# One decoder layer on one NeuronCore: w_down over all eight PSUM banks, with seven block products in place of eight for six of sixteen pairs of contraction tiles

## The reference, cut to what matters

```python
x = x + merged @ w_out                                  # (256, 2048)
hn = rms_norm(x, norm_mlp)                              # gain, and a factor per token
x = x + jnp.square(jax.nn.relu(hn @ w_up)) @ w_down     # w_up (2048, 8192), w_down (8192, 2048)
```

## Time and profile before

| | before |
|---|---|
| median of three runs | 1338.79 us (1338.76 to 1339.06) |
| the profiled execution: span from the first to the last instruction | 1337.1 us |
| TensorE busy | 1333.2 us, 6034 matmuls |
| VectorE busy | 961.8 us |
| ScalarE busy | 652.0 us |
| GpSimd busy | 14.9 us |
| granted TensorE clock, mean over the core's activity | 1.000 of full |
| read from memory | 256.46 MB, 193 GB/s |

### The profile page before, as it was taken

How to read it: one execution, slowest core, us unless ns; L and a number is a source line. 1 busy time by engine, 2 the same in 40 slices (tenths; PEclk the granted TensorE clock), 3 DMA queues, 4 the chain that set the end, 5 groups by cost and what they waited for, 6 DMA issues and landing times.

```text
span 1337.1 us, 16355 instructions
## 1 busy us (share of the span) xinstructions
PE 1333.2 (100%) x6034; PEld 1109.3 (83%) x6034; DVE 961.8 (72%) x1333; ACT 652.0 (49%) x797; POOL 14.9 (1%) x30
## 2 busy tenths in 40 slices
PE   9999999999999999999999999999999999999999
PEld 7988888888888888888888888888888888888887
DVE  6788699777487875999787878444546878764453
ACT  6656544656445444454545454343335454543332
POOL 0101000000000000000000000000000000000000
PEclk9999999999999999999999999999999999999999
DMA  9656565555556755564656565555566665555552
GB/s 317 206 172 220 190 203 164 186 186 164 183 161 217 252 197 184 186 220 163 215 189 198 182 213 180 201 188 191 196 196 197 191 192 188 191 197 198 197 191 95
DMA packets 131829, 259.35 MB, mean 194 GB/s; under 512 B 4366, under 2 KB 7484, under 8 KB 131516
## 3 DMA queue, kind: packets, MB, share of 16 engines
q1 hardware_dynamic: 131740, 258.57, 58.5%
q10 hardware_dynamic: 32, 0.01, 0.0%
HBM read 256.46 MB, written 2.10 MB: 193 GB/s over the span
## 4 chain that ended last, share of the span: by engine, by line
PE 99%; DMA 0%; SPq 0%; DVE 0%; issue 0%
PE ps L1100 31%; PE ps L1102 31%; PE ps L1101 31%; PE ps L1190 1%; PE ps L1171 1%; PE ps L1139 1%; PE ps L1135 1%; PE ps L1137 1%; PE ps L1145 0%; DMA rows<-in_x_dram 0%; PE ps L1210 0%; PE ps L1227 0%; PE ps L1209 0%; PE ps L1238 0%; PE ps L1120 0%; PE ps L1254 0%
## 5 line engine op out<-in xcount | busy, mean ns | idle before, releaser
L697 DVE TENSOR_TENSOR w_lo<-raw,w_hi 128x1024 fp32r<-128x1024 f32 (+1 forms) x477 | 581.0, 1224 | 337.7 <-ACT w_hi L429 333.5
L429 ACT ACTIVATE w_hi<-raw 128x1024 fp32r<-128x1024 f32 (+1 forms) x477 | 503.8, 1061 | 584.8 <-PE ps L1102 575.6
L1100 PE MATMUL ps<-w_hi,xT 128*128 128x512 f32 x1088 | 425.8, 391 | 0.0
L1102 PE MATMUL ps<-w_hi,xT 128*128 128x512 f32 x1088 | 423.5, 389 | 0.0
L1101 PE MATMUL ps<-w_lo,xT 128*128 128x512 f32 x1088 | 423.3, 389 | 0.0
L1102 PEld LDWEIGHTS ps<-w_hi,xT 128*128 128x128 f32 x1088 | 204.2, 188 | 42.8
L1100 PEld LDWEIGHTS ps<-w_hi,xT 128*128 128x128 f32 x1088 | 204.3, 188 | 41.9
L1101 PEld LDWEIGHTS ps<-w_lo,xT 128*128 128x128 f32 x1088 | 204.3, 188 | 41.7
L1100 PE MATMUL ps<-w_hi,branch 128*128 128x512 f32 x384 | 149.4, 389 | 0.0
L1101 PE MATMUL ps<-w_lo,branch 128*128 128x512 f32 x384 | 149.4, 389 | 0.0
L1102 PE MATMUL ps<-w_hi,branch 128*128 128x512 f32 x384 | 149.4, 389 | 0.0
(11 more groups left out here) (199 smaller groups left out, 582.0 us busy)
## 6 DMA issues: line engine op xcount, KB each, us to landing
raw<-in_w_in_dram SPq DMA_DIRECT2D x73, 1024.0 KB, 5.1
raw<-in_w_up_dram SPq DMA_DIRECT2D x64, 1024.0 KB, 5.8
raw<-in_w_down_dram SPq DMA_DIRECT2D x64, 1024.0 KB, 5.0
raw<-in_w_out_dram SPq DMA_DIRECT2D x16, 1024.0 KB, 5.1
raw<-in_w_branch_b_dram SPq DMA_DIRECT2D x8, 1024.0 KB, 5.0
raw<-in_w_branch_a_dram SPq DMA_DIRECT2D x8, 1024.0 KB, 5.1
raw<-in_w_in_dram SPq DMA_DIRECT2D x4, 1040.0 KB, 8.7
rows<-in_x_dram SPq DMA_DIRECT2D x1, 2048.0 KB, 10.1
```

The lines of the kernel that those rows point to most:

```text
L429: act.activation(dst[:, k % RING, :, :], src[:, k // 2, KH * (k % 2):KH * (k % 2) + KH, :], ACT.Copy).then_inc(hi_made, 1)
L697: dve.tensor_tensor(lo[:, k % RING, :, :], src[:, k // 2, KH * (k % 2):KH * (k % 2) + KH, :], hi[:, k % RING, :, :].bitcast(F32), ALU.subt ...
L1100: pe.matmul(o, hi, w_hi[:, s, i, :], start=first, stop=False)
L1102: last = pe.matmul(o, lo, w_hi[:, s, i, :], start=False, stop=end)
```

## The change

The down stage of each half f is done in two blocks n of 1024 columns instead of four of 512. A block has 16 pairs of contraction tiles, taken in a written order (`ORDER`), and SyncE loads one pair of tiles by 1024 columns (1 MB) per slot. TensorE adds up into all eight banks: four of the block's own (two token halves by two column halves), four shared ones for the other kind of pair.

Ten of the pairs are whole pairs: two steps of one tile by 1024 columns, 12 matmuls each, as many as before. The six others (`SEVEN`) take the pair of tiles, the two token halves and the two column halves as a 2 by 2 block product and do it with seven block products instead of eight: four steps with 6, 3, 6 and 6 matmuls. For this the weights need four sums (w1 - w0, w3 - w1, w3 less the first, w2 less the third). GpSimd makes them with three TENSOR_TENSOR instructions per pair (two sums of 512 in one of 1024 elements, and two of 512), into `w_diff` and in place in the raw slot. ScalarE and VectorE split 1024, 512, 1024 and 1024 elements for the four steps; steps 2 and 3 wait for GpSimd (`diff_made`). The features need four sums too: VectorE makes them (five instructions of 128 elements per pair, in the up stage), and ScalarE and VectorE split them (two instructions each).

The four shared banks are combined and added into `rows` by VectorE (`add_shared`), and the own banks by `add_own`. The factor of the token is no longer applied at these adds but at the Relu, as its square root (`x2_r`, from GpSimd), and the Relu is two instructions of 512 instead of one of 1024. The loops of the MLP are written out. The end of the last block is cut as before, with two 256-wide pieces last. The diff, cut:

```diff
 B_UP = B_OUT + NN
-FB = 16
+SEVEN = (3, 5, 7, 9, 11, 13)
+ORDER = ((0, 1, 2, 4, 3, 6, 5, 8, 7, 10, 9, 12, 11, 13, 14, 15), (0, 3, 1, 5, 2, 7, 4, 9, 6, 11, 8, 13, 10, 12, 14, 15))
+PARTS = [[4 if i in SEVEN else 2 for i in ORDER[n]] for n in range(2)]
+DOWN = sum(PARTS[0]) + sum(PARTS[1])
+FB = 8 + DOWN // 8
...
+        w_diff = gate_f[:, 0:1024]
+        part_sums = gate_f.rearrange("p (a n) -> p a n", n=N)
...
+        def step_of(f, n, at, part=0):
+            return 8 * (B_UP + FB * f + 8) + (sum(PARTS[0]) if n else 0) + sum(PARTS[n][:at]) + part
...
+                for n in range(2):
+                    for at, i in enumerate(ORDER[n]):
+                        k = at % RAW
+                        if n == 0 and at < RAW:
+                            sp.wait_ge(lo_made, 8 * (B_UP + FB * f + 7) + 2 * k + 2)
+                        else:
+                            was = (n, at - RAW) if at >= RAW else (0, 16 + at - RAW)
+                            sp.wait_ge(lo_made, step_of(f, *was) + PARTS[was[0]][was[1]])
+                        sp.dma_start(raw[:, k, :, :].rearrange("p (a b) n -> p a (b n)", b=2),
+                                     w_down_t[:, 32 * f + 2 * i:32 * f + 2 * i + 2, 2 * N * n:2 * N * n + 2 * N])\
...
+                    before = None
+                    for at, i in enumerate(ORDER[n]):
+                        if i not in SEVEN:
+                            continue
+                        k, made = at % RAW, diffs_before(f, n, at)
+                        q = raw[:, k, :, :]
+                        pool.wait_ge(landed[k], 16 * (B_UP + 16 * f + 8 + 4 * n + at // RAW) + 16)
+                        if before is not None:
+                            pool.wait_ge(lo_made, before + 1)
+                        else:
+                            if n == 0:
+                                pool.wait_ge(up_squared, 8 * f + 8)
+                            if n == 1 or f == 1:
+                                pool.wait_ge(shared_read, 2 * f + n)
+                        pool.tensor_tensor(diffs, q[:, 1:4:2, :], q[:, 0:2, :], ALU.subtract).then_inc(diff_made, 1)
+                        pool.wait_ge(diff_made, made + 1)
+                        link(pool.tensor_tensor(q[:, 1, :], q[:, 3, :], diffs[:, 0, :], ALU.subtract))
+                        pool.wait_ge(lo_made, step_of(f, n, at) + 1)
+                        pool.tensor_tensor(q[:, 2, :], q[:, 2, :], q[:, 1, :], ALU.subtract).then_inc(diff_made, 1)
+                        before = step_of(f, n, at, 2)
...
+            def down_hi(f, s):
+                n, at, part = place_of(f, s)
+                g, k = step_of(f, n, at, part), at % RAW
+                flat = raw[:, k, :, :].rearrange("p t n -> p (t n)")
+                dst = w_hi[:, g % RING, :, :].rearrange("p t n -> p (t n)")
+                if PARTS[n][at] == 2:
+                    src = flat[:, 1024 * part:1024 * part + 1024]
+                else:
+                    src = (flat[:, 1024:2048], flat[:, 0:N], w_diff, flat[:, N:N + 1024])[part]
+                if part == 0:
+                    act.wait_ge(landed[k], 16 * (B_UP + 16 * f + 8 + 4 * n + at // RAW) + 16)
+                elif part >= 2:
+                    act.wait_ge(diff_made, diffs_before(f, n, at) + part - 1)
+                act.wait_ge(w_used, g - RING + 1)
...
+                    for m in range(M):
+                        last = act.activation(up_pos[:, N * m:N * m + N], ps[:, 4 + 2 * u + m, :], ACT.Relu,
+                                              scale=x2_r[:, m:m + 1])
+                    last.then_inc(up_read, 1)
...
+                if at == 0 and 2 * j - 1 in SEVEN:
+                    q, t = SEVEN.index(2 * j - 1), 4 * j - 2
+                    act.wait_ge(pair_sum, len(SEVEN) * f + q + 1)
+                    act.activation((branch, merged)[t // 16][:, t % 16, 0, P:S], sums[:, 0, :], ACT.Copy)
+                    act.activation(sum_ops(2 * j - 1)[:, :, 0, :], sums[:, 1:4, :], ACT.Copy).then_inc(pair_hi, 1)
...
+                        if 8 * blk0 + i == step_of(f, n, last_shared(n), 3) + 3:
+                            act.wait_ge(w_used, step_of(f, n, last_shared(n), 3) + 1)
+                            act.activation(part_sums[:, 0, :], ps[:, SHARED[n], :], ACT.Copy).then_inc(first_kept, 1)
...
+                if at == 7 and 2 * j + 1 in SEVEN:
+                    a11, a21, a12, a22 = (ps[:, 2 * u + 1, P * c:P * c + P] for c in range(4))
+                    link(dve.tensor_copy(sums[:, 3, :], a21))
+                    dve.tensor_tensor(sums[:, 2, :], a11, sums[:, 3, :], ALU.subtract)
+                    link(dve.tensor_tensor(sums[:, 0, :], sums[:, 3, :], a22, ALU.add))
+                    link(dve.tensor_tensor(sums[:, 1, :], sums[:, 0, :], a11, ALU.subtract))
+                    dve.tensor_tensor(sums[:, 3, :], a12, sums[:, 1, :], ALU.subtract).then_inc(pair_sum, 1)
+                if at == 1 and 2 * j - 1 in SEVEN:
+                    q, t = SEVEN.index(2 * j - 1), 4 * j - 2
+                    dve.wait_ge(pair_hi, len(SEVEN) * f + q + 1)
+                    a, ops = (branch, merged)[t // 16][:, t % 16, :, P:S], sum_ops(2 * j - 1)
+                    dve.tensor_tensor(a[:, 1, :], sums[:, 0, :], a[:, 0, :].bitcast(F32), ALU.subtract)
+                    dve.tensor_tensor(ops[:, :, 1, :], sums[:, 1:4, :], ops[:, :, 0, :].bitcast(F32),
+                                      ALU.subtract).then_inc(pair_lo, 1)
...
+            def add_shared(f, n, late_part):
+                b, r0, r1 = SHARED[n], out_rows(0, n), out_rows(1, n)
+                if not late_part:
+                    dve.wait_ge(first_kept, 2 * f + n + 1)
+                    link(dve.tensor_tensor(part_sums[:, 2, :], part_sums[:, 0, :], ps[:, b + 2, :], ALU.add))
+                    dve.tensor_tensor(part_sums[:, 1, :], part_sums[:, 2, :], ps[:, b + 1, :], ALU.add)
+                    link(dve.tensor_tensor(part_sums[:, 3, :], part_sums[:, 2, :], ps[:, b + 3, :], ALU.add))
+                    link(dve.tensor_tensor(r1.rearrange("p (a n) -> p a n", a=2), r1.rearrange("p (a n) -> p a n", a=2),
+                                           part_sums[:, 3, :].unsqueeze(1).to_broadcast([P, 2, N]), ALU.add))
+                else:
+                    dve.tensor_tensor(r1[:, N:2 * N], r1[:, N:2 * N], ps[:, b + 1, :], ALU.add)
+                    link(dve.tensor_tensor(r0, r0, part_sums[:, 0:2, :].rearrange("p a n -> p (a n)"), ALU.add))
+                    dve.sem_inc(shared_read, 1)
...
+            def add_own(f, n):
+                dve.wait_ge(w_used, step_of(f, n, 15, 1) + 1)
+                for m in range(M):
+                    r, b = out_rows(m, n), OWN[n] + 2 * m
+                    dve.tensor_tensor(r, r, banks(b, b + 2), ALU.add).then_inc(down_read, 1)
...
+            def three(bank, a_hi, a_lo, w_at, start, end, cols=slice(0, N), out=slice(0, N)):
+                s, c = w_at
+                pe.matmul(ps[:, bank, out], a_hi, w_hi[:, s, c, cols], start=start, stop=False)
+                pe.matmul(ps[:, bank, out], a_hi, w_lo[:, s, c, cols], start=False, stop=False)
+                return pe.matmul(ps[:, bank, out], a_lo, w_hi[:, s, c, cols], start=False, stop=end)
...
+            def whole_pair(f, n, at):
+                i = ORDER[n][at]
+                for part in range(2):
+                    g = step_of(f, n, at, part)
+                    pe.wait_ge(lo_made, g + 1)
+                    for m in range(M):
+                        if n == 0 and at == 0 and part == 0:
+                            pe.wait_ge(up_read, 8 * f + 7 + m)
+                        a = feature(2 * i + part, m)
+                        for c in range(2):
+                            last = three(OWN[n] + 2 * m + c, a[:, 0, :], a[:, 1, :], (g % RING, c), at == 0 and part == 0,
+                                         at == 15 and part == 1 or (f, n, at, part, m, c) == (1, 1, 14, 1, 1, 1))
+                    last.then_inc(w_used, 1)
+            def seven_pair(f, n, at):
+                i = ORDER[n][at]
+                own, shared = OWN[n], SHARED[n]
+                first, end = PARTS[n][:at].count(4) == 0, at == last_shared(n)
+                a11, a21, a12, a22 = (feature(2 * i + t, m) for t in range(2) for m in range(M))
+                s1, ops = a21, sum_ops(i)
+                s2, s3, s4 = (ops[:, c, :, :] for c in range(3))
+                g = step_of(f, n, at)
+                pe.wait_ge(lo_made, g + 1)
+                three(own, a12[:, 0, :], a12[:, 1, :], (g % RING, 0), False, False)
+                three(own + 1, s4[:, 0, :], s4[:, 1, :], (g % RING, 1), False, False).then_inc(w_used, 1)
+                g += 1
+                pe.wait_ge(lo_made, g + 1)
+                if first and n == 0:
+                    pe.wait_ge(up_lo_made, 8 * f + 8)
+                elif first:
+                    pe.wait_ge(down_read, 4 * f + 2)
```

(69 more changed lines are left out.)

225 lines of the change are left out of this document (107 added, 118 removed).

## The result

The changed kernel takes 1360.43 us (median, 1360.09 to 1360.78) against 1338.78 for the kernel before on the same chip: the ratio is 1.0162, with a 95% interval of 1.0148 to 1.0177. It is 21.6 us slower; 12.1 were forecast.

The account below looks back on a forecast made before the run. The prediction took TensorE, busy over the whole span, to bound the kernel. Its terms, -16.3 + 2.4 + 26 = +12.1 us, took 1338.8 to 1350.9 us, with a range of 1324 to 1362.

Parts of the forecast that it names:

- Fewer matmuls: Down stages: 21 matmuls in place of 24 in each of 24 seven pairs, 72 fewer at 0.2266 us, -16.3 us.
- The bank wait: First down step: TensorE waits 1.2 us for the last Relu to read the shared banks, twice, +2.4 us.
- The rings without GpSimd: Short steps of seven pairs: the 2.7 us chain through ScalarE and VectorE fits in 3.4 us, cost 0.
- GpSimd's sums: Down stages: sums and VectorE's splits exclude each other, so together they outlast the matmuls and delay TensorE, +26 us.
- The price of 4.7 us: GpSimd's time for the three sums of a seven pair, 2.3 + 1.2 + 1.2 us, with ends 2.3 and 5.4.
- The turn of 0.19 us: Down stages: each change between VectorE's splits and GpSimd's sums adds 0.19 us, three times per seven and whole pair.
- The period of 11.5 us: One seven and one whole pair: splits, sums and turns one after the other, against 10.2 us of matmuls.
- took off 6.9 us per block: Down blocks: two sums made before (3.5) and three splits made ahead (3.4) reduce the lateness.
- The 31 us: GpSimd's sums if, beyond 23 us, each of 24 seven pairs loses the full 1.3 us at step 3.
- A (splits not held): Down stages: only GpSimd waits, VectorE's splits are never held by sums; 1324.9 us, chance 0.28.
- B (cheap sums): Down stages: exclusion holds, but sums take only 2.3 us a pair, deciding below 3.4; 1327 us, chance 0.09.
- C (short steps late by themselves): Seven pairs: signals or ScalarE's waits exceed the spare time by 0.5 us, losing 12 us without exclusion; 1337 us, chance 0.08.

Follow-up runs that it names:

- e6: The kernel before with 24 unneeded GpSimd additions of 1024 elements in each down stage, with no data going between them and the splits; 1338.80 us.
- e2: The changed kernel with each GpSimd sum replaced by two memsets of the same destination, which write without reading; 1327.73 us.
- e4: The changed kernel with all three sums made by VectorE and the last up block's Relu put ahead of one high part on ScalarE; 1327.69 us.
- e1: The changed kernel with GpSimd's three sums per seven pair cut to 8 elements each, all waits kept; 1327.26 us.
- e10: The changed kernel, all three sums on GpSimd, with the start of the long one moved behind the split of step 3; 1350.35 us.
- e9: The changed kernel with the two 512 sums on VectorE and GpSimd's long sum started one split later; 1359.92 us, against 1343.04 without the later start.
- e7: The changed kernel with each GpSimd sum replaced by two one-input copies to the same destination; 1336.82 us.

## Why the prediction was right, and by how much it was off

**The direction and the mechanism held.** The forecast took it that splits and sums exclude each other both ways, where the trace before showed one way; e6 shows the other, with nothing else between the two. The Trainium skill's page "SBUF — State Buffer" (Who interferes with whom) says that the second of the two waits for the whole instruction, and that writing alone doesn't matter. e2 agrees, with no split longer. e6 agrees to within about 0.1 us: the split took 1.62 us more than its 1.23, and ended 1.10 behind the addition.

**Fewer matmuls, -16.3:** 5962 as said. **The bank wait, +2.4:** 1.2 us at each down stage, and 2.1 back in e4.

**The rings without GpSimd, 0:** no wait on a split in e1, so the chain fits as said. But this step missed the wider spacing inside seven pairs, +2.4 us.

**GpSimd's sums, +26:** this term was too small; it measures 1360.43 - 1327.26 = 33.2 us, and it came this near by errors that offset each other.

- The price of 4.7 us for the three sums, the middle between two readings of the earlier trace rows, stands against 2.41 + 1.29 + 1.29 = 4.99. The middle had no ground but caution, so its nearness is luck. With 4.99 in its place the forecast's own sum gives about 29 instead of 23.
- The turn of 0.19 us between the engines has the wrong sign: in e10 splits and sums take 0.4 us less than their sum of 11.24, not 0.57 more. One after the other they need 10.83 us, not 11.5.
- The period of 11.5 us stands against 11.44, but for another reason: VectorE is idle for 3.0 of the 11.44. The forecast had taken the place of the long sum, ahead of step 3's split, for a few us on top of its capacity sum; it is over half of the loss in a period, and 10.1 us of the whole (e10).
- The forecast took off 6.9 us per block for two sums and three splits made ahead. From the first matmul of a block's first seven pair to the end of its last one it so had 57.7 us in block 0 and 60.0 in block 1; the trace after has 59.9 and 63.7, and e1, without sums, 50.9 and 56.4. The sums were made ahead (818.17 and 820.68), the splits were not: when TensorE starts the first seven pair, at 834.80, VectorE has just begun the split of its step 1, since it turned the last up block until 834.63. How much of the missing time is this and how much the place was not measured.

The 31 us that the forecast gave as the most (24 pairs times 1.3) is nearer to 33.2, but it isn't how the loss is made up: a period loses 1.1, and a block's first pair and the step behind it lose 2 to 3.

**The sum:** 1338.8 - 16.3 + 2.4 + 2.4 = 1327.3 against 1327.26 in e1, which is the test of the first terms. The 33.2 is the difference of two runs, so that with it the sum comes to 1360.5 by construction (measured 1360.4). Forecast 1350.9, range 1324 to 1362: the measured time lies near its upper end. The rivals: A (splits not held) is refuted by e6; B (cheap sums) by 4.99 us a pair, above the 3.4 from which it would have held; C (short steps late by themselves) by e1.

The signs named came: splits start where a sum ends, TensorE idles 0.68 us by the record behind a seven pair (0.84 by the starts of its matmuls), and a down stage takes over 174 us.

## What to carry to other kernels

Work handed to GpSimd that reads SBUF, beside VectorE instructions with two inputs there, is not free even when GpSimd is idle: add its time to VectorE's, and ask which step VectorE is late for while the longest of them runs. If the same work takes half as long on VectorE and fits in its gaps, leave it there. A capacity sum is a lower bound only: with a ring of a few short steps, moving one long reader by one split changed the time by 10 us down (e10) or 17 us up (e9).

## What the runs showed of the hardware that had not been expected

- A GpSimd subtraction of float32 takes 2.41 us for 128x1024 and 1.29 for 128x512, a copy 1.04 and 0.61, a memset 0.96 and 0.53 (after, e7, e2). Those that read hold off a two-input VectorE instruction and are held by it; a memset does neither.
- Some 0.1 us of a GpSimd instruction overlaps with VectorE: in e10 the splits (6.25 us) and the three sums (4.99 alone) fit into 10.83 us, 0.14 less per sum, and in e6 a held split of 1.23 ends 1.10 us after the addition.
- The one that starts first holds the other, if only by 20 ns (e9): the same long sum, started behind the same split, held the next two splits for 2.3 us in e9 and was itself held for 0.86 in e10.
- Matmuls that are all alike, 128x512 with weights loaded for each, start 0.2266 us apart. In a seven pair five starts lie 0.24 apart (e1), three of them behind the first matmul with a summed feature or at a change between feature buffers, without any wait on record. Why was not tried.
